# Attention scores of a two-layer encoder step: two products over 128 rows in place of three or four

## The reference, cut to what matters

```python
# layer 0, per head pair
s = einsum('bqhd,bkhd->bhqk', q, k) * 64 ** -0.5          # q, k rotated
p = softmax(where(k_pos // 64 <= q_pos // 64, s, -inf))
a = p[:, :, 0] - lam * p[:, :, 1];  o = rmsnorm(a @ v)
# layer 1, per head
s = einsum('bqhd,bkhd->bhqk', q, k) * 64 ** -0.5
s = s + cq[..., :, None] - ck[..., None, :]                # c = cumsum(log_sigmoid(f))
p = softmax(where(k_pos <= q_pos, s, -inf));  o = p @ v
```

## Time and profile before

| | |
|---|---|
| time, median of 3 runs | 1629.19 us (1623.55 to 1631.59) |
| span of the profiled execution | 1627.6 us |
| PE busy, share of the span | 97% |
| DVE, ACT, POOL busy | 38%, 37%, 37% |
| chain that ended last, share by engine | PE 86%, DVE 6%, issue 3%, ACT 3% |
| mean granted TensorE clock | 0.984 |
| mean DMA rate | 76 GB/s |

### The profile page before, as it was taken

The page is one execution under the profiler, slowest core; times in us unless marked ns, Lnnn a source line. Parts: engine busy times, 40 slices in busy tenths (PEclk is TensorE's granted clock), DMA queues, the critical chain, the costliest instruction groups (busy, mean ns, idle before and its releaser), DMA issues.

```text
span 1627.6 us, 29919 instructions
## 1 busy us (share of the span) xinstructions
PE 1571.9 (97%) x11071; PEld 1484.0 (91%) x11071; DVE 613.6 (38%) x1075; ACT 604.4 (37%) x1059; POOL 605.6 (37%) x292
## 2 busy tenths in 40 slices
PE   6999999999999999999999999999999999999996
PEld 6778888899999999999978888888999999999996
DVE  5566666553111111121355666565431111111212
ACT  5466666543222222222334444444342222222221
POOL 3333334234445444433322222222344544544331
PEclk9899999999999999999999999999999999999998
DMA  4122112112222222222221111211122222222222
GB/s 164 61 74 81 63 60 71 56 65 78 81 87 77 86 82 77 82 85 84 91 82 61 61 60 60 63 56 47 65 66 89 77 81 87 77 84 78 81 84 81
DMA packets 41555, 123.76 MB, mean 76 GB/s; under 512 B 4624, under 2 KB 9232, under 8 KB 41504
## 3 DMA queue, kind: packets, MB, share of 16 engines
q1 hardware_dynamic: 41504, 123.06, 22.5%
HBM read 111.21 MB, written 11.83 MB: 76 GB/s over the span
## 4 chain that ended last, share of the span: by engine, by line
PE 86%; DVE 6%; issue 3%; ACT 3%; DMA 0%; SPq 0%; POOL 0%; DVEq 0%; ACTq 0%; POOLq 0%
PE ps L487 70%; PE sps L537 3%; PE ops L600 2%; PE tps L557 2%; PE sps L543 2%; PE sps L539 2%; PE sps L538 2%; DVE qf L1242 1%; PE sps L545 1%; PE ops L590 1%; DVE acc L1200 1%; ACT qsw L836 1%; DVE qf L1215 1%; PE tps L571 1%; DVE aug_l L1328 1%
## 5 line engine op out<-in xcount | busy, mean ns | idle before, releaser
L1096 POOL TENSOR_TENSOR w_lo<-w_raw,w_hi 128x1024 fp32r<-128x1024 f32 (+1 forms) x199 | 470.9, 2367 | 851.5 <-ACT w_hi L796 851.5
L487 PE MATMUL ps<-xh,w_hi 128*128 128x288 f32 x2176 | 491.5, 308 | 20.8 <-DVE xl L1443 11.8
L487 PE MATMUL ps<-xh,w_lo 128*128 128x288 f32 x2176 | 470.0, 298 | 0.0
L487 PE MATMUL ps<-xl,w_hi 128*128 128x288 f32 x2176 | 469.7, 298 | 0.0
L796 ACT ACTIVATE w_hi<-w_raw 128x1024 fp32r<-128x1024 f32 (+1 forms) x200 | 208.3, 1042 | 451.9 <-PE ps L487 449.4
L487 PEld LDWEIGHTS ps<-xh,w_hi 128*128 128x128 f32 x2176 | 351.8, 192 | 22.9 <-issue 22.1
L487 PEld LDWEIGHTS ps<-xh,w_lo 128*128 128x128 f32 x2176 | 354.5, 191 | 0.0
L487 PEld LDWEIGHTS ps<-xl,w_hi 128*128 128x128 f32 x2176 | 354.2, 191 | 0.0
L887 ACT ACTIVATE pr<-sps,nmax 128x384 f32<-128x384 f32 (+3 forms) x160 | 86.0, 538 | 189.1 <-DVE nmax L1258 171.7
L487 PE MATMUL ps<-hh,w_lo 128*128 128x288 f32 x704 | 150.9, 295 | 0.0
L487 PE MATMUL ps<-hl,w_hi 128*128 128x288 f32 x704 | 150.8, 295 | 0.0
(11 more groups left out here) (155 smaller groups left out, 1845.7 us busy)
## 6 DMA issues: line engine op xcount, KB each, us to landing
w_raw<-w_units SPq DMA_DIRECT2D x184, 512.0 KB, 3.2
w_raw<-w_units SPq DMA_DIRECT2D x16, 384.0 KB, 2.9
xT<-x_in SPq DMA_DIRECT2D x8, 288.0 KB, 5.7
dk_out<-kf SPq DMA_DIRECT2D x8, 288.0 KB, 2.1
dv_out<-vf SPq DMA_DIRECT2D x8, 288.0 KB, 4.0
fk_out<-kf SPq DMA_DIRECT2D x8, 288.0 KB, 4.1
fv_out<-vf SPq DMA_DIRECT2D x8, 288.0 KB, 4.0
y_out<-yt SPq DMA_DIRECT2D x8, 288.0 KB, 2.3
```

Source lines behind the costliest of these rows:

```text
L487: mm = nc.tensor.matmul(out[:, half, :], w[:, k, :], rhs[:, kt, half * HALF:(half + 1) * HALF], start=start and w is w_hi[slot] and rhs is ...
L1096: nc.gpsimd.tensor_tensor(w_lo[slot][:, 0:kts, :], w_raw[slot][:, 0:kts, :], w_hi[slot][:, 0:kts, :].bitcast(F32), ALU.subtract).then_inc( ...
```

## The change

Each 64-row half of a head pair gets its own 128-row operand. In `qa[:, h]` the half's own 64 rows hold the high part of q and the other 64 rows its low part; in `ka[:, h]` the high part of k stands in both halves, written once by ACT and copied to the other 64 rows by a DMA of SP. One product over 128 rows then gives high*high + low*high. The second product multiplies with `kb`, whose own rows hold the low part of k; the other rows are zero in the first layer. In the second layer they hold the negated cumulated sums and ones, and `qb` carries the high part of q in its own rows and the selected cumulated sums in the others, so that the same second product adds the bias. `kb` has one buffer, so `k_lo` waits for the last score of the pair before, and in the second layer moves from slot 12 to 17; there the last six score jobs move up by one or two slots. Activations and subtractions that handled 128 rows in one instruction become two of 64 rows, `q_hi` of the second layer four.

```diff
-S_AT = {DIFF: [0, 1, 3, 4, 7, 8, 11, 12, 15, 16], FOX: [0, 1, 3, 5, 8, 10, 12, 14, 16, 18]}
+S_AT = {DIFF: [0, 1, 3, 4, 7, 8, 11, 12, 15, 16], FOX: [0, 1, 3, 5, 7, 9, 11, 13, 15, 16]}
...
-K_LO_AT = {DIFF: 17, FOX: 12}
+K_LO_AT = {DIFF: 17, FOX: 17}
...
+            def copy_k_hi(L, g):
+                slot = g.c % 2
+                sp.wait_ge(kh_done, val(g + (G * L + 1)))
+                sp.dma_start(ka[slot][64:128, 0, :].bitcast(F32), ka[slot][0:64, 0, :].bitcast(F32)).then_inc(k_copied, 16)
+                sp.dma_start(ka[slot][0:64, 1, :].bitcast(F32), ka[slot][64:128, 1, :].bitcast(F32)).then_inc(k_copied, 16)
+
+            def load_aug_r():
+                sp.wait_ge(f_step, 12)
+                sp.wait_ge(kb_clear, 4)
+                for h in range(2):
+                    for i in range(2):
+                        r, q = 64 - 64 * h + 32 * i + 16, 64 - 64 * h + 32 * i
+                        sp.dma_start(kb[r:r + 16, h, :].bitcast(F32), ncum[q:q + 16, :]).then_inc(aug_r_loaded, 16)
...
                 if second and L == FOX:
                     sp.wait_ge(f_step, 5)
                     sp.dma_start(lf_out, lf[0:2 * G, 0:T]).then_inc(lf_stored, 16)
+                    load_aug_r()
                 if not start:
                     load_unit(u + 1)
                 if not first:
                     store_k(L, g - 1)
+                    copy_k_hi(L, g - 1)
...
-                    for s in (qh_done, ql_done, kh_done, kl_done):
+                    for s in (qh_done, ql_done, kl_done):
                         pe.wait_ge(s, val(a + (G * L + 1)))
-                nc.tensor.matmul(out, qh[par][b, q], kh[par][b, k], start=True, stop=False)
-                nc.tensor.matmul(out, qh[par][b, q], kl[par][b, k], start=False, stop=False)
-                nc.tensor.matmul(out, ql[par][b, q], kh[par][b, k], start=False, stop=False)
-                if L == FOX:
+                    pe.wait_ge(k_copied, val((a + (G * L + 1)) * 32))
+                nc.tensor.matmul(out, qa[par][:, h, q], ka[par][:, h, k], start=True, stop=False)
+                if L == DIFF:
+                    nc.tensor.matmul(out, qa[par][:, h, q], kb[:, h, k], start=False, stop=False)
+                else:
                     pe.wait_ge(aug_l_done, val(a * 2 + (h + 1)))
-                    nc.tensor.matmul(out, aug_l[h][:, q], aug_r[:, k], start=False, stop=False)
+                    if jj == 0:
+                        pe.wait_ge(aug_r_loaded, 64)
+                    nc.tensor.matmul(out, qb[par][:, h, q], kb[:, h, k], start=False, stop=False)
...
             def k_hi(L, g, par):
-                nc.scalar.activation(kh[par][:], kf[:], ACT.Copy).then_inc(kh_done, 1)
+                nc.scalar.activation(ka[par][0:64, 0, :], kf[0:64, :], ACT.Copy)
+                nc.scalar.activation(ka[par][64:128, 1, :], kf[64:128, :], ACT.Copy).then_inc(kh_done, 1)
...
             def q_hi(L, g, par):
-                nc.scalar.activation(qh[par][:, 0:T], qf[:], ACT.Copy, scale=QK_SCALE).then_inc(qh_done, 1)
+                if L == FOX:
+                    nc.scalar.activation(qb[par][0:64, 0, 0:T], qf[0:64, :], ACT.Copy, scale=QK_SCALE)
+                    nc.scalar.activation(qb[par][64:128, 1, 0:T], qf[64:128, :], ACT.Copy, scale=QK_SCALE)
+                nc.scalar.activation(qa[par][0:64, 0, 0:T], qf[0:64, :], ACT.Copy, scale=QK_SCALE)
+                nc.scalar.activation(qa[par][64:128, 1, 0:T], qf[64:128, :], ACT.Copy, scale=QK_SCALE
+                                     ).then_inc(qh_done, 1)
...
             def k_lo(L, g, par):
                 dve.wait_ge(kh_done, val(g + (G * L + 1)))
-                tt(kl[par][:], kf[:], kh[par][:].bitcast(F32), ALU.subtract).then_inc(kl_done, 1)
+                if some(g + G * L):
+                    dve.wait_ge(s_done, val((g + G * L) * 10))
+                for h in range(2):
+                    r = slice(64 * h, 64 * h + 64)
+                    op = tt(kb[r, h, :], kf[r, :], ka[par][r, h, :].bitcast(F32), ALU.subtract)
+                op.then_inc(kl_done, 1)
...
             def q_lo(L, g, par):
                 dve.wait_ge(qh_done, val(g + (G * L + 1)))
-                stt(ql[par][:, 0:T], qf[:], QK_SCALE, qh[par][:, 0:T].bitcast(F32), ALU.mult, ALU.subtract
-                    ).then_inc(ql_done, 1)
+                for h in range(2):
+                    r, o = slice(64 * h, 64 * h + 64), slice(64 - 64 * h, 128 - 64 * h)
+                    op = stt(qa[par][o, h, 0:T], qf[r, :], QK_SCALE, qa[par][r, h, 0:T].bitcast(F32),
+                             ALU.mult, ALU.subtract)
+                op.then_inc(ql_done, 1)
...
             def aug_left(g):
                 for h in range(2):
-                    if later(g):
-                        dve.wait_ge(s_done, val((g + (G - 1)) * 10 + 5 * (h + 1)))
-                    nc.vector.tensor_scalar(aug_l[h][:], aug_m[:], column(head_sel, g * 2 + h), None, ALU.mult
-                                            ).then_inc(aug_l_done, 1)
+                    dve.wait_ge(s_done, val((g + (G - 1)) * 10))
+                    r = slice(64 - 64 * h, 128 - 64 * h)
+                    nc.vector.tensor_scalar(qb[g.c % 2][r, h, 0:T], aug_m[r, :], column(half_sel[r, :], g * 2 + h), None,
+                                            ALU.mult).then_inc(aug_l_done, 1)
```

## The result

The changed kernel takes **1646.81 us** (median; 1646.19 to 1647.55), beside 1626.64 (1623.55 to 1631.59) for the kernel before on the same chip: ratio 1.0113, 95% interval 1.0089 to 1.0137. The forecast was 1647. The profiled span is 1643.9 us, 16.3 more than before, at a mean granted clock of 0.969 (before 0.984).

The account below looks back on a forecast made before the run. TensorE bounds each pair up to its last score, then a serial chain. Terms 15 + 8 + 4.6 - 10 = +17.6 on the 1627.6 us span give 1645; the median standing 1.6 higher, 1647 us, spread 1630 to 1663.

Parts of the forecast that it names:

- The chain behind the last score sets the periods: Both layers: work between a pair's last score and the next first score bounds the first layer and nearly the second.
- Rival A: Both layers: TensorE stays the bound and its 90 us saving arrives in full, 1539 us; chance 0.08.
- step (1): First layer: only TensorE's saving before the fourth score moves the chain forward, -1.4 us a pair.
- Steps (2) to (4): First layer, per pair: second halves of `k_hi` +0.4, of `k_lo` beside GpSimd +1.1, of `q_hi` and `q_lo` +1.3 us.
- The clock, +0.8 on average: First layer: the longer wait before the first score drops the clock in every pair, not every second; +0.8 us.
- First layer's periods, +15: First layer: +2.2 us a pair including the clock, over seven periods, +15 us.
- Second layer, +1.1 a pair: Second layer: period 39.5 against 39.88 us, plus 1.5 for the clock; net +1.1 a pair, +8 over seven periods.
- Starts: First pairs: first layer +2.1 us, second layer +2.5 (0 to 5); copies of high k cost nothing.
- Ends, -10: Last pair of each layer: no next q follows, so TensorE keeps its saving, -10 us (of 11.3).
- Rival B: Second layer: `k_lo` not cut by w_lo, `take_q` 2.4 us earlier, period 37.1 not 41.0, 1620 us; chance 0.2.
- Rival D: Score blocks: the passage cost between row heights stays, 0.28 us a block lost, 1657 us; chance 0.07.
- Rival C: Both layers: clock stays low longer than a single drop, another 2.2 us over fourteen pairs, 1678 us; chance 0.1.

Follow-up runs that it names:

- e1: Changed kernel with the second layer's two `k_lo` halves moved from slot 17 to slot 23, behind `take_q`; 1625.46 us, ratio 0.9977.
- e5: Changed kernel with second-layer VectorE order changed: `k_lo` in slot 20, `q_lo` and forget bias in slot 23; 1621.42 us, ratio 0.9950.
- e9: e5 with the two products that make the second layer's forget bias moved to slot 14; 1604.19 us, ratio 0.9843.
- the fill: Unneeded products before each first-layer pair's first score: 18 in the changed kernel, 1635.67 us; eight in the kernel before, 1619.29 us.
- e4: Kernel before, products unchanged, with first-layer high and low parts of q and k made in two 64-row instructions each; 1665.95 us, ratio 1.0227.
- e6: Changed kernel with the first layer's two `k_hi` halves moved from slot 14 to 16, behind the last two scores' exponentials; 1647.38 us, ratio 1.0108.
- e2: Changed kernel with pair 0's copies of high k issued ahead of the cumulated bias transfers at the second layer's start; 1643.82 us, ratio 1.0087.
- e3: Changed kernel with GpSimd making only one eighth of one w_lo a pair in the second layer, from pair 2 on; 1633.74 us, ratio 1.0030.
- e8: Changed kernel with the first layer's ScalarE weight split for the next pair moved from slot 18 to 22, so w_lo follows; 1648.82 us, ratio 1.0113.

## Why the prediction was right, point by point

**The chain behind the last score sets the periods: shown.** The same products gave 41.35 and 34.94 us in the second layer, by the order on VectorE alone (e1, e5, e9). Rival A's saving was there: 7.0 us a pair was TensorE's share of it, and 5.0 arrived (39.92 to 34.94) once the chain was out of the way. The kernel before was not run with the new order, but in the same stage its TensorE is busy for 237.59 of 239.54 us at a clock of 1.00, so the order alone could have given it some 0.3 us a pair:

```profile
871.77:1111.31 239.54, 237.59 (x1567) 204.81 (x1566) 145.01 (x318) 107.54 (x264) 54.83 (x25) 1.00 0.20 61
```

**First layer, step (1), -1.4.** With the fill on both sides the change costs 1.1 (36.16 against 35.05). The halves cost 2.6 (e4), so the products gave 1.5, by subtraction: near -1.4. The reason given, that VectorE and ScalarE pass the work to and fro and let TensorE wait, has no run of its own; e6 agrees with it, where the exponentials only changed what they waited for.

**Steps (2) to (4), +0.4, +1.1, +1.3.** In e4 0.3, 1.1 and 1.2. `k_lo` was stretched from 2.2 to 3.4 by GpSimd, as said.

**The clock, +0.8 on average.** The fill gives back 1.7 a pair in the changed kernel and 0.8 in the one before: +0.9 for the change. The wait that causes it was forecast at 6 to 8 us before the first score. It is 6.3, but in three places: 1.97, 0.87 and 3.50. The first two are in front of the last transpose and of the products with v. The remainder that the transpose needs is made at 261.06, ahead of `k_lo`, and comes late by ScalarE, where its high part (260.65) stands behind the two of `k_hi`, the exponentials and a swap; the remainder that the products need (264.85) stands behind `k_lo` on VectorE. The prediction had such waits for the second layer only.

**First layer's periods, +15: mis-sized.** The last six grew by 2.04 each (2.2 forecast), but the first one, 38.24 before, shrank to 35.34, and the sum is 9.35. The term multiplied by seven what held for six. The kernel before ran that first pair at 0.52 for long; the changed kernel has 0.75 in the same stretch:

```profile
44.00:54.00 10.00, 8.21 (x48) 6.91 (x48) 5.79 (x11) 5.22 (x11) 4.05 (x2) 0.75 0.37 123
```

With the fill the first period is 34.00 in the kernel before and 34.76 in the changed one: filling takes 4.2 off the one and 0.6 off the other. So the step that was left out is the clock of this one pair. Why it comes back earlier in the changed kernel is open; in runs with the same first layer the first period lies between 35.3 and 36.8.

**Second layer, +1.1 a pair.** Measured +1.4 over the last six, and 8.3 in all (8 forecast): the last score at 22.7 (22.8 forecast), `k_lo` cut by w_lo (4.27), `take_q` at 30.05, waits of 2.90 and 3.31 ahead of the last transposes, the clock at 0.94, as the prediction listed them. The tail was forecast at 9.1 and 1.5 for the clock; it is 11.0.

**Starts: the step that failed.** The prediction gave the copies of k nothing, since ten slots cover them, and the second layer's start 2.5 (0 to 5). The cover is there in every pair but one: in the second layer's first, the copies stand on SP behind the wait for the cumulated bias, which the prediction named only for the load of unit 4. TensorE waits 10.52 for them, and the start is 9.2 late (5.66 more from the last first score of the first layer, and the 3.6 that TensorE saves there: its last matmul ahead of the wait ends 6.7 later than before, at 834.1, where that first score was 10.3 later). "Or if TensorE waits for the copies" stood among what would make it wrong, and at this place it was. With the copies first (e2) the start is 3.6 late, inside the forecast's 0 to 5. The first layer's start, +2.1, measured +0.9; in other runs with the same first layer the first score comes 1.7 to 2.9 later than in the kernel before.

**Ends, -10.** -3.6 and -8.0: 11.6, all of what TensorE saves there (11.3 forecast).

So the sum was 17.6 and came out at 16.2, with two errors of opposite sign: the second layer's start 6.7 too low, the first layer's first period 5 too high or so. The mechanism was right; the agreement to a microsecond is partly luck. It also stands on 1629.19 us for the kernel before: beside the median of 1626.64 the change costs 20.2 us, beside the profiled spans 16.3.

**Rival B** named its point rightly, whether w_lo starts between the halves of `k_lo`, and its direction (e3), but its price was twice too high: without the cut the period fell by 1.9, not by 3.9, because a wait of up to 3.3 us on `ptl` a pair stayed, and with it a clock of 0.95. Rival D is out by the blocks (0.47 saved each). Rival C is out as a cost of every pair: in the first layer the clock is whole again some 3.5 us after a first score. At the second layer's beginning it did stay low for longer (0.51 from 878.5 to 889).

## What to carry to other kernels

When work is taken off the busiest engine, write down the chain that the next stage's first operation waits for, and count every instruction that the change puts into it, before counting the saving. Then order each engine by what that chain needs: here three moves within the same work turned +1.1% into -1.6% (e9). Work that needs nothing of the running stage (the bias) or that is needed only at the end (`k_lo`) goes out of the chain first. Look at each queue not only for the steady pair but for the one pair in which something else stands on it: there a transfer that is hidden everywhere else is in the open.

## What the runs showed of the hardware that was not expected

- **An op of VectorE that is split in two can let a whole GpSimd op in between.** Two halves of `k_lo` took 2.17 (e1) and 2.19 (e9) alone, 3.41 with a product of 1.43 beside them, 4.27 with a w_lo of 2.76; two bias products took 1.06 alone and 3.05 with a w_lo that began 0.25 before them. In e1 and e9 no GpSimd op fell between them, but for one pair of e1; in e5 a move put the next w_lo ahead of other ops, and moving w_lo itself made TensorE wait for it (e8). The Trainium skill, "SBUF — State Buffer", Who interferes with whom, says that the first to issue holds the port for a whole instruction; these rows agree (the first half of `k_lo` kept its 1.08 though w_lo had asked), and add that GpSimd got it at the next boundary between VectorE's instructions.
- **Products that nobody needs made the kernels faster**: 18 in each first-layer pair took 11 us off the changed kernel, 8 took some 9 off the one before, since the granted clock stayed at 1.00 in place of 0.50.
- Products of 128 rows that follow one another cost 0.18 us each at 384 columns, the start of the next included. The load of the second product's weights (244.40) runs beside the first product, both over all 128 rows. The Trainium skill, "TensorE: Matmul & The Clock Gate", The mechanism (in Part 3), says that a weight load overlaps running matmuls only where the row groups differ, though it names a background weight buffer beside that; the rows show the overlap without different row groups, and the measurement decides.
